# HGRN2's diagonal gram as 32x32 products on four places, and twelve projection passes moved from ahead of the sum of squares to the head's end

## What is computed

```
def gla_chunkwise(q, k, v, log_f):
    ...
    def step(S, inp):
        q_c, k_c, v_c, lf_c = inp
        bc = jnp.cumsum(lf_c, axis=2)
        diff = bc[:, :, :, None, :] - bc[:, :, None, :, :]
        dec = jnp.exp(jnp.where(mask, diff, -jnp.inf))
        scores = jnp.einsum('bhtd,bhsd,bhtsd->bhts', q_c, k_c, dec)
        o = (jnp.einsum('bhts,bhsv->bhtv', scores, v_c)
             + jnp.einsum('bhtd,bhdv->bhtv', q_c * jnp.exp(bc), S))
        ...

def hgrn2_mixer(hn, w_in, lower_bound, norm_w, w_out):
    q, f, i, g = jnp.split(hn @ w_in, 4, axis=-1)
    q = jax.nn.silu(q)
    fg = lower_bound + (1.0 - lower_bound) * jax.nn.sigmoid(f)
    k = 1.0 - fg
    log_f = jnp.log(fg)
    o = gla_chunkwise(q, k, i, log_f)          # 8 heads, 128 channels each
    o = o * lax.rsqrt(jnp.mean(o * o, -1, keepdims=True) + RMS_EPS)
    o = o.reshape(b, s, HGRN_WIDTH) * norm_w * jax.nn.silu(g)
    return o @ w_out
```

## Time and profile before

| | |
|---|---|
| median of 3 runs | 2862.8 us (2859.31 to 2864.19) |
| the profiled execution | 2866.67 us |
| its span, first to last instruction | 2864.9 us |
| TensorE busy over the span | 2560.0 us, 89% |
| VectorE busy | 1927.5 us, 67% |
| ScalarE busy | 1603.4 us, 56% |
| mean granted TensorE clock | 0.942 |

### The profile page before, as it was taken

How to read it: one execution, slowest core, us unless ns; L and a number is a source line. 1 busy time by engine, 2 the same in 40 slices (tenths; PEclk the granted TensorE clock), 3 DMA queues, 4 the chain that set the end, 5 groups by cost and what they waited for, 6 DMA issues and landing times. The chain is left out here.

```text
span 2864.9 us, 57992 instructions
## 1 busy us (share of the span) xinstructions
PE 2560.0 (89%) x20884; PEld 2091.0 (73%) x20884; DVE 1927.5 (67%) x2201; ACT 1603.4 (56%) x1867; POOL 381.3 (13%) x342
## 2 busy tenths in 40 slices
PE   5998899978979999999658999999698999999990
PEld 4776789947758888888547787777585788888870
DVE  3358355534479999999555666666535899999974
ACT  3656223253248888888424555555312888888861
POOL 0020000000003333333110000000000222222220
PEclk8999999999989999999869999999897999999995
DMA  3111000013259999999531111111323999999964
GB/s 96 45 44 30 27 4 4 4 60 122 94 197 378 381 385 384 380 377 378 193 119 31 31 38 31 38 34 49 106 87 120 338 376 376 382 384 384 383 256 189
DMA packets 219991, 525.39 MB, mean 183 GB/s; under 512 B 43824, under 2 KB 99120, under 8 KB 219824
## 3 DMA queue, kind: packets, MB, share of 16 engines
q1 hardware_dynamic: 201392, 489.34, 46.1%
q0 software_dynamic: 18432, 33.60, 3.1%
HBM read 506.06 MB, written 50.33 MB: 194 GB/s over the span
## 5 line engine op out<-in xcount | busy, mean ns | idle before, releaser
L1754 DVE TENSOR_TENSOR w_low<-w_raw,w_high 128x1024 fp32r<-128x1024 f32 x768 | 895.0, 1221 | 30.0 <-DVEq L52 20.2
L1467 ACT CAST w_high<-w_raw 128x1024 fp32r<-128x1024 f32 x768 | 755.3, 1050 | 107.3 <-ACTq L52 105.7
L1622 PE MATMUL ps<-w_high,x_high 128*128 128x512 f32 x1024 | 414.7, 405 | 7.1 <-PEq L52 6.2
L1626 PE MATMUL ps<-w_high,x_low 128*128 128x512 f32 x1024 | 403.3, 394 | 0.0
L1625 PE MATMUL ps<-w_low,x_high 128*128 128x512 f32 x1024 | 401.6, 392 | 0.0
L1622 PEld LDWEIGHTS ps<-w_high,x_high 128*128 128x128 f32 x1024 | 194.9, 190 | 50.3 <-issue 13.7
L1626 PEld LDWEIGHTS ps<-w_high,x_low 128*128 128x128 f32 x1024 | 194.0, 189 | 43.3
L2027 PE MATMUL ps<-h_high,w_high 128*128 128x512 f32 x512 | 215.5, 421 | 11.2 <-PEq L52 11.1
L1625 PEld LDWEIGHTS ps<-w_low,x_high 128*128 128x128 f32 x1024 | 194.7, 190 | 37.6
L1622 PE MATMUL ps<-w_high,hidden_high 128*128 128x512 f32 x512 | 200.8, 392 | 6.7 <-PEq L52 6.7
L2027 PE MATMUL ps<-h_low,w_high 128*128 128x512 f32 x512 | 203.9, 398 | 0.0
(11 more groups left out here) (410 smaller groups left out, 4872.3 us busy)
## 6 DMA issues: line engine op xcount, KB each, us to landing
w_raw<-in_moe_w_gate SPq DMA_DIRECT2D x256, 512.0 KB, 5.3
w_raw<-in_moe_w_up SPq DMA_DIRECT2D x256, 512.0 KB, 5.7
w_raw<-in_moe_w_down SPq DMA_DIRECT2D x256, 512.0 KB
w_raw<-expert_rows SPq DMA_DIRECT2D x32, 512.0 KB, 9.3
w_tiles<-in_c_w_in SPq DMA_DIRECT2D x32, 512.0 KB, 4.0
w_tiles<-in_ab_w_in SPq DMA_DIRECT2D x22, 512.0 KB, 3.9
residual<-in_x SPq DMA_DIRECT2D x16, 512.0 KB, 6.8
h_rows<-hn_moe SPq DMA_DIRECT2D x16, 512.0 KB, 2.8
```

Source lines behind the costliest of these rows:

```text
L1467: act.copy(wh[:, p, :], raw[:, p, :]).then_inc(high_made, 1)
L1622: ins = pe.matmul(ps[:, bank, :], high, w_h, start=first, stop=False)
L1626: return pe.matmul(ps[:, bank, :], low, w_h, start=False, stop=final)
L1754: dve.tensor_tensor(wl[:, p, :], raw[:, p, :], wh[:, p, :].bitcast(F32), ALU.subtract).then_inc(low_made, 1)
```

## The change

Three edits. The diagonal gram of a head was eight products of 128x128 and is now 32 products of 32x32: only the squares on the diagonal of each block are made, and four successive products write to partitions 0, 32, 64 and 96 (the four places). They go to the same places in PSUM as before; VectorE's pick is as it was. The call ahead of the sum of squares asks for 4 triples, not 8, and the call behind it for 13, not 9, which covers all that is left; so twelve passes move behind the sum. And the eight semaphores of the output rows become five, one for each slot of the ring, waited for at 16 and then at 32.

```diff
-        out_in = [sem(f"out_in{k}") for k in range(KT)]
+        out_in = [sem(f"out_in{k}") for k in range(RING)]
...
-                    sp.dma_start(ring[:, k % RING, :], w_out[k * P:(k + 1) * P, :]).then_inc(out_in[k], 16)
+                    sp.dma_start(ring[:, k % RING, :], w_out[k * P:(k + 1) * P, :]).then_inc(out_in[k % RING], 16)
...
                 def gram(left, right):
                     for b in range(2):
                         take(pe, gram_free[b])
-                        for n in range(4):
-                            t = slice((4 * b + n) * P, (4 * b + n + 1) * P)
-                            last = pe.matmul(ps[:, 4 + b, n * P:(n + 1) * P], left[:, t], right[:, t], start=True, stop=True)
+                        for n in range(0, 4 * P, 32):
+
+                            t = slice(4 * b * P + n, 4 * b * P + n + 32)
+                            last = pe.matmul(ps[n % P:n % P + 32, 4 + b, n:n + 32], left[:, t], right[:, t], start=True, stop=True)
                         last.then_inc(gram_done[b], 1)
...
                     last.then_inc(s["o_done"], 1)
-                    project(8)
+                    project(4)
                     take(pe, s["sq_ready"])
                     for h in range(NH):
                         last = pe.matmul(ps[:, 6 + h, :], c.ones[:], KD[:, h * HALF:(h + 1) * HALF], start=True, stop=True)
                     last.then_inc(s["sq_summed"], 1)
-                    project(9)
+                    project(13)
...
-                        act.wait_ge(out_in[k], 16)
+                        act.wait_ge(out_in[k % RING], 16 * (k // RING + 1))
```

## The result

The changed kernel takes 2846.18 us (median of 5 runs, 2843.94 to 2853.21) against 2863.03 us before. The ratio is 0.9947, with a 95% interval of 0.9932 to 0.9962: 15 us faster, between 11 and 19. The forecast was 2846.5; that the two medians agree to 0.3 us is in part luck, since the interval is 8 us wide.

A forecast was written before the change was run, and what follows sets the result against it. A head was bound by TensorE's work, the hole before the gram and the slow clock after it. Six borders' 14.6 us plus 1.7 at the last made 16.3: 2862.8 becomes 2846.5 us, range 2840 to 2854.

The forecast's parts named there:

- The twelve passes: At each border, the sum comes earlier; variance and gram move 0.92 us, the pick 0.34, with a 0.5 us stall.
- The gram: Diagonal gram on TensorE: 64 records of 32x32 take 0.8 us in place of 2.25 us.
- The two bounds: Limits for the new gram's time: 0.66 us from a similar row, 2.5 us with no overlap of places.
- The clock: Behind the borders: with the hole at 0.7 us, full clock throughout; a half-clock stretch costs 1.6 us of TensorE's work.
- The gate: Ahead of level gram 0, the diagonal pick frees bank 4 after TensorE arrives; 1 us of hole returns, border wins 2.4.
- The last border and the ends: Into head 7, without low(0), Ln starts 1.7 us earlier and head 7 takes it whole; head 0 counts nothing.
- (b): Rival: the clock still drops after each border; 1.85 us a border won, 2850 us; chance 0.14.
- (c): Rival: places don't overlap at 32 columns, gram 2.5 us; 2850.4, or 2860 with slow clock; chance 0.09 for both.
- e: Rival: each 32x32 record takes 0.14 us like a 128x128 one, gram 9.0 us; slower, 2896 us; chance 0.03.
- (f): Rival: squares come late and the stall at the sum grows; about no change, 2860 to 2863 us; chance 0.03.
- (d): Rival: smaller stall at the sum or G copy not held; 3.0 us a border, 2843 us; chance 0.07.

The follow-up runs named there:

- e5: Changed kernel with the gram's small products sorted by place, four in a row writing to the same one; 2846.74 us, ratio 0.9942.
- e4: Changed kernel with VectorE's pick of the diagonal moved ahead of low(1), which waits for ScalarE's high(1); 2841.48 us, ratio 0.9922.
- e9: Kernel before plus two dummy products on TensorE behind the turn of V, filling the hole before the gram; 2855.94 us, ratio 0.9978.
- e3: Kernel before with only the five semaphores for the eight rows of output weights, old gram and old passes; 2859.33 us, ratio 0.9999.
- e1: Kernel before with only the small gram (64 records of 32x32), passes where they were; 2855.36 us, ratio 0.9973.
- e6: Changed kernel with no pass ahead of the sum of squares, 17 triples behind it; 2863.62 us, ratio 1.0008.
- e2: Kernel before with only the twelve passes moved behind the sum, gram of 128x128 products kept; 2847.70 us, ratio 0.9949.
- e7: Changed kernel with 18 passes (six triples) ahead of the sum of squares, 11 triples behind it; 2846.78 us, ratio 0.9939.
- e11: The kernel of e10 with 15 passes ahead of the sum of squares instead of 12; 2837.21 us, ratio 0.9917.
- e10: The kernel of e4 with the variance on VectorE also moved ahead of low(0); 2835.68 us, ratio 0.9919.

## Why the prediction was right

**The twelve passes.** Right in mechanism, a little off in size. The variance was to start at 6.8 on this scale and starts at 6.79; the gram's load was to go 0.92 us earlier and goes 0.93 earlier. The stall at the sum was put at 0.5 us and is 0.4: I had taken VectorE's handover of 0.27 us for ScalarE too, and ScalarE's took 0.11 (1711.95 to 1712.06). The last pass was to end 0.5 us later and ends only 0.2 later on this scale (13.28 against 13.06), so the pick moved 0.63 us, not 0.34. The turn of V too ended sooner than worked out (13.91, not 14.20), so the hole before the gram, between loads, shrank to 0.9 to 1.3 us and not to 0.7. Why the last pass lost less than the whole stall is not shown.

**The gram.** 0.8 us forecast, 0.75 measured. The two bounds were 0.66 and 2.5; e5 shows that even without turns over the places it is 1.4. e4 and e5 together show why the size did not matter. The twelve passes with the entry into the level gram were put at 2.95 us; where nothing holds them, in e4, they take 2.93 to 2.97.

**The clock.** The forecast, no half clock at the borders, held, and e9 shows that it was worth 1.7 us each. The wider sentence, the full clock throughout, did not hold: head 7 got a half-clock stretch, and this in the very rows whose full clock before had been read as the argument against a fall. It cost nothing that can be seen there. To this extent the right forecast at the borders was luck. What makes the clock fall is not settled. It fell at all six borders before with a hole of 2.1 us and a 128x128 gram, at five of six in e3 with the same program there, at three of six in e1 with the same hole, and at none in e6 with a hole of 2.8 us ahead of the sum. Ahead of head 7's gram the hole is 2.0 us in the kernel before, in e1 and in e3, and the clock fell behind it in e1 alone. So the length of a hole alone does not decide. Where the hole before the gram was 1.3 us or less (the changed kernel, e2, e4, e5, e7, e9 to e11) no border of a profiled execution had it.

**The gate.** The sum put a border at 2.4 us and it is 2.8 (22.15 to 19.35): the term was mis-sized by the 0.3 us of the pick just named, and little else. For the same reason the gate returned 0.5 to 0.8 us and not 1.0.

**The last border and the ends.** The variance of head 6 starts 2.07 us earlier and the first pick of head 7 1.74 us (17.45 to 15.71), forecast 1.7. Head 0 was counted at nothing. It took 71.7 us from gram to gram against 71.4, although its own border won 0.93: the half clock covered more of the twelve passes behind its level gram 0, and they took 4.87 us instead of 3.59. That is not the change's doing as far as the runs show: e3, with the old program, took 72.2 us there, and e5, with the new gram and the moved passes, 70.6. From the first gram of head 1 to that of head 7 it is 370.6 us against 388.9, and head 7 with its tail 53.9 against 53.8. So 18.3 less 0.3 and 0.1: 17.8 us, where 16.3 was forecast. The timed medians are 16.9 apart.

**Rivals.** The half clock at the borders (b), slow small records (c, e) and a loss at the sum (f) did not come. (c)'s premise was half true, the size was not. (f) is real: e6 is that case. (d), more gain because the stall is smaller, is what happened in part.

## What to carry to other kernels

Lay a repeating stage over itself from one fixed instruction, and write down when each of the engines' handovers comes; then a change's gain is the distance from the old latest arrival among the things that the next step needs to the new latest one, and not the sum of what was shortened. Here TensorE came last before, at 22.1, and the pick comes last now. Two parts that shorten the way to one gate are worth little more than the better one, and what then stands at the gate, a copy queued behind an unrelated wait, is often free to move. Work put ahead of a wait should be just enough to cover it: twelve or eighteen passes were alike here, with 24 the variance came 0.9 us later, and with none the whole gain was lost.

## What the hardware showed that I had not expected

- Adding two useless products to TensorE made the kernel 6 us faster (e9, between 3 and 9), with the full clock at all six borders. What the clock is worth shows in e3: the one border that kept it had level gram 0 at 20.53, the others at 22.13 to 22.16, 1.6 us.
- The same border, instruction for instruction, fell to the half clock every second time (e1), and an idle time of 2.8 us between dense stretches did not bring it (e6). What decides it stays open.
- fp32 records of 32x32 follow each other at 12 ns over four places, 20 ns over two and 22 ns when four in a row share a place.
- At the borders behind the loop's branch the gram of e10 starts up to 1.1 us late, although the multiply that frees the banks has ended 1.1 us before. Instruction loads fall into that time (two in the 9 us there), but as many do in e4, whose gram, due 0.8 us later, starts on time there (14.84). That they are the cause was not tried.
